# The last eight gate tiles move from between the delta levels to in front of the delta chain

## What is computed

```
u = rms(x, norm_mix)
dn_qkv, dn_z, dn_b, dn_a, r_*, a_*, i_*, gate = split(u @ w_in)      # gate: 3 x 1024 columns
c = silu(causal_conv(dn_qkv)); q, k, v = split(c); q, k = l2norm(q), l2norm(k)
o_a = chunked_recurrence(q, k, v, g, beta, dn_s0)                    # delta rule
# in a chunk: a = I + strict_lower(k k^T * decay * beta); solve a @ [u, kcum] = [v*beta, k*beta*exp(G)]
#             w = u - kcum @ s;  o = qd @ s + qk @ w;  s = s*gt + kd^T @ w
h = x + w_o @ sum_n sigmoid(gate_n) * (branch_n @ w_branch_n)
y = h + conv_ffn(rms(h))
```

## Time and profile before

| | us |
|---|---|
| median of three executions | 3210.27 |
| the profiled execution, its own time | 3210.03 |
| its span, first to last instruction | 3208.2 |
| PE busy in the span | 2894.5 (90%) |
| DVE busy | 1485.8 (46%) |
| ACT busy | 1258.8 (39%) |
| POOL busy | 812.5 (25%) |
| mean granted TensorE clock | 0.918 of 2.4 GHz |

### The profile page before, as it was taken

How to read it: one execution, slowest core, us unless ns; L and a number is a source line. 1 busy time by engine, 2 the same in 40 slices (tenths; PEclk the granted TensorE clock), 3 DMA queues, 4 the chain that set the end, 5 groups by cost and what they waited for, 6 DMA issues and landing times. The chain is left out here.

```text
span 3208.2 us, 56817 instructions
## 1 busy us (share of the span) xinstructions
PE 2894.5 (90%) x22582; PEld 2719.8 (85%) x22582; DVE 1485.8 (46%) x2238; ACT 1258.8 (39%) x2255; POOL 812.5 (25%) x364
## 2 busy tenths in 40 slices
PE   4998999989986989999879999899889879899996
PEld 3998988888876979999868989788878769799995
DVE  2362855654433526436136448466444243461541
ACT  3431434751113435345244224367311053552542
POOL 1221222220000424444222213122100024244441
PEclk7998999999975989999979979999999589899998
DMA  5221324533323513232232222254333234123321
GB/s 166 80 83 57 100 88 146 165 104 100 96 67 95 187 53 93 73 106 68 79 96 82 64 79 91 97 183 126 116 90 97 79 121 151 53 81 98 87 83 58
DMA packets 366310, 315.86 MB, mean 98 GB/s; under 512 B 42710, under 2 KB 314488, under 8 KB 365494
## 3 DMA queue, kind: packets, MB, share of 16 engines
q10 hardware_dynamic: 257332, 188.09, 19.7%
q1 hardware_dynamic: 108706, 124.05, 13.1%
HBM read 273.70 MB, written 38.38 MB: 97 GB/s over the span
## 5 line engine op out<-in xcount | busy, mean ns | idle before, releaser
L757 POOL TENSOR_TENSOR w_lo<-w_raw,w_hi 128x1024 fp32r<-128x1024 f32 (+2 forms) x360 | 812.3, 2257 | 2339.0 <-ACT w_hi L1343 2339.0
L764 PE MATMUL big<-uhi,w_hi 128*128 128x272 f32 x3968 | 1208.4, 305 | 62.7 <-DVE ulo L1845 24.4
L766 PE MATMUL big<-uhi,w_lo 128*128 128x272 f32 x3968 | 1165.0, 294 | 0.0
L765 PE MATMUL big<-ulo,w_hi 128*128 128x272 f32 x3968 | 1159.6, 292 | 0.0
L764 PEld LDWEIGHTS big<-uhi,w_hi 128*128 128x128 f32 x3968 | 765.2, 193 | 123.3 <-issue 71.8
L765 PEld LDWEIGHTS big<-ulo,w_hi 128*128 128x128 f32 x3968 | 768.2, 194 | 3.7 <-issue 1.9
L766 PEld LDWEIGHTS big<-uhi,w_lo 128*128 128x128 f32 x3968 | 764.9, 193 | 0.0
L1343 ACT ACTIVATE w_hi<-w_raw 128x1024 fp32r<-128x1024 f32 (+2 forms) x360 | 343.8, 955 | 346.1 <-PE big L766 317.3
L764 PE MATMUL big<-hhi,w_hi 128*128 128x272 f32 x704 | 204.8, 291 | 1.4 <-DVE hlo L2376 1.4
L766 PE MATMUL big<-hhi,w_lo 128*128 128x272 f32 x704 | 203.6, 289 | 0.0
L765 PE MATMUL big<-hlo,w_hi 128*128 128x272 f32 x704 | 202.9, 288 | 0.0
(11 more groups left out here) (351 smaller groups left out, 4111.9 us busy)
## 6 DMA issues: line engine op xcount, KB each, us to landing
w_raw<-in_w_in ACTq DMA_DIRECT2D x66, 1024.0 KB, 5.6
w_raw<-in_w_up ACTq DMA_DIRECT2D x88, 512.0 KB, 5.0
kpage<-in_cache_k SPq DMA_DIRECT2D x128, 256.0 KB, 3.1
w_raw<-in_w_down ACTq DMA_DIRECT2D x32, 704.0 KB, 4.8
d_conv<-in_cache_v SPq DMA_DIRECT2D x64, 256.0 KB, 2.7
d_pad<-in_cache_v SPq DMA_DIRECT2D x64, 256.0 KB, 2.6
gate_dram<-gate_raw ACTq DMA_DIRECT2D x48, 272.0 KB, 2.2
sig<-gate_dram SPq DMA_DIRECT2D x48, 272.0 KB, 3.4
```

The source lines that it names most:

```text
L757: po.tensor_tensor(split_view(lo, t), tile_of(t), split_view(hi, t).bitcast(F32), ALU.subtract).then_inc(w_lo.sem, w_lo.next(t))
L764: pe.matmul(out, wh, xh, start=start, stop=False)
L765: pe.matmul(out, wh, xl, start=False, stop=False)
L766: return pe.matmul(out, wl, xh, start=False, stop=stop)
```

## The change

The last eight gate tiles join `DN_PHASE` behind the last delta projection. There they are ordinary dense tiles, each at one go, in alternating slots (`DN_SLOT`), with `store_gate` behind each. `TILES`, and so the order in which weights are loaded and split, stays the same. The generator and all `advance` calls go from the delta chain, and both `store_gate` calls from ACT's part of it. Nothing stands in their place. `silu_of(11)` moves from behind the whole list to ahead of the first added gate copy. The value pages stay where they are. `key_slot` does nothing at the added positions, since all key pages are done by then. The core of the diff:

```diff
-DN_PHASE = dn_with_gates('dn0', 'dn1', 'dn2', *GATES[4:6]) + dn_with_gates('dn3', 'dn4', 'dn5', *GATES[6:8])
-DELTA_GATES = [(u, i) for u in GATES[8:12] for i in range(2)]
+DN_PHASE = dn_with_gates('dn0', 'dn1', 'dn2', *GATES[4:6]) + dn_with_gates('dn3', 'dn4', 'dn5', *GATES[6:8]) \
+    + [(u, i) for u in GATES[8:12] for i in range(2)]
@@ TensorE
-        gates = gate_steps(DELTA_GATES)
         for c in range(5):
@@ the prologue, after two value pages
-                advance(gates, 8)
@@ in each level, after Y and after YT
-                    advance(gates, 1)
@@ after the levels, after kc, after the first part of do
-                advance(gates, 3)
-                advance(gates, 5)
-                advance(gates, 2)
@@ ACT, in the loop over DN_PHASE
+            if p == DN_AT[-1] + 1:
+                silu_of(11)
             if u in GATES:
                 store_gate(u, j, p % 2)
@@ ACT, the chain
-        silu_of(11)
         for c in range(5):
-                if c < 4 and s == LEVELS[4]:
-                    store_gate(*DELTA_GATES[2 * c], 1)
-                store_gate(*DELTA_GATES[2 * c + 1], 1)
```

More of the change, by code:

```diff
@@ L217 @@
     + [(u, i) for u in UNITS[UIDX['ak0']:UIDX['dn0']] for i in range(2)] + DN_PHASE \
-    + [(u, i) for u in UNITS[UIDX['dn5'] + 1:] for i in range(2)]
+    + [(u, i) for u in UNITS[UIDX['br00']:] for i in range(2)]
 TIDX = {t: i for i, t in enumerate(TILES)}
@@ L1203, in _ @@
                     value_page(next(pages))
-                    advance(gates, 1)
-            if c < 4:
-                advance(gates, 3)
             pe.wait_ge(X[0].drained, X[0].at(('YT', c, levels[-1])))
```

## The result

The changed kernel took **3245.97 us**, the median of four executions (3242.96 to 3249.27), beside 3210.18 for the kernel before on the same chip (four, 3208.25 to 3211.61). The ratio is 1.0112, 95% interval 1.0095 to 1.013: slower by 36 us. The forecast was 3236, range 3219 to 3258. The profiled execution is the longest of the four, 3249.27 us with a span of 3247.5, 3.3 us above its median; differences between profiles are read with that in mind.

What follows compares the result with a forecast made beforehand. TensorE was busy nearly everywhere but not always the bound; within levels, TensorE, ACT and DVE take turns. 48.3 - 8.3 - 20.0 - 12.1 = +7.9 us a layer; 3210.03 + 15.8 + 10 (clock) = 3236 us, range 3219 to 3258.

Steps and rivals of the forecast that it cites:

- Part 1: Ahead of the chain: eight added dense gate tiles at 6.04 us each, +48.3 us a layer.
- Part 2: The head, before the first level: TensorE's idle and half-clock start go, 8.3 us instead of 16.6, -8.3 us a layer.
- Parts 3 and 4: Levels and chunk end: gate steps on the path go, 5.0 us a chunk over four chunks, -20.0 us a layer.
- Part 5: Prologues of chunks 1 to 3: 9.7 us instead of 15.7, 14.3 and 11.3, without POOL's w_lo and gate steps, -12.1 us a layer.
- Part 6: TensorE's clock in prologues and around kc: four falls to half clock taken, +10 us, range 0 to +30.
- A: Chunk 4 and sample states: clock stays up behind the chain, so not slower, 3189 us; 4%.
- A2: Chain: no clock dips, and the 0.20 us idle ahead of the gate step goes too, 3218 or 3215 us; 11%.
- B: Levels: without gate steps the clock falls, 2.5 us in each of 56 levels, +140, near 3365 us; 5%.
- C: Level and chunk ends: something other than gate steps orders them, the chain gives half, +20, near 3256 us; 8%.
- D: Dense tiles: ACT is crowded, a tile takes 7 us instead of 6.04, +15 in both layers, 3251 us; 5%.

Runs made afterwards that it cites:

- the kernel with the held clock: The changed kernel plus 30 matmuls a chunk whose results nobody reads, ahead of dvT, ahead of the first level and around kc: 3231.8 us.
- the two runs that move it: Four tiles in free chain places, next weights prepared right behind the gate store: 3184.4 us; the kernel before, preparation moved two levels into the next chunk: 3191.81 us.
- the kernel of before with the deferred preparation: The kernel before, with the weight preparation after the second store of chunks 0 to 2 moved two levels into the next chunk: 3191.81 us.
- the run on chunk 4: The kernel with four gate tiles in free chain places, plus 42 matmuls in chunk 4 whose results nobody reads: 3186.83 us.
- the kernel with five tiles: Against the kernel with four gate tiles in free chain places, a fifth put in the chain, three left dense: 3175.15 us.

## Why the prediction was right in sign and range, and 10 us short

- **Part 1, the dense tiles: right.** 8 x 6.04 is 48.3; measured 48.1 (702.41 to 750.55).
- **Part 2, the head: right.** From the first grow matmul to the first Y 7.65 us, forecast 8.3. With part 1 the stretch ahead of the first Y grew by 39.2 us, forecast 40.0.
- **Parts 3 and 4, levels and chunk end: right, slightly too high.** Read in the kernel with the held clock, chunk 3 to dS is 36.57 us where it was 41.1: 4.5 us, forecast 5.0. A level gives 0.38 us, where I kept 0.42. The 0.20 us that TensorE's queue takes behind a page is still there, now ahead of Y.
- **Part 5, the prologues: right.** dS to Y 9.65 to 9.75 us, forecast 9.7; 12.2 us a layer, forecast 12.1. That POOL's `w_lo` was the cause of the 2.41 us copy is shown by the two runs that move it, together with the ends of the copies.
- Parts 1 to 5 together: 39.2 - 4 x 4.54 - 12.2 = +8.8 us a layer, +18 in both, where the forecast was +15.8.
- **Part 6, the clock: the step that was mis-sized.** I took four falls at 2.5 us, +10, from gaps of 1 and 1.9 us against one of 2.91 that had made the clock fall. The kernel before had shown a second such case that I did not use: the clock fell behind a gap of 2.88 us in chunk 2's prologue (0.50 from 823.86 to 827.27), and not behind the 1.38 us of chunk 3's, where eight gate steps follow. Now it fell twelve times, the upper bound that I had written down, and all eight prologues were among them. The price of one was below mine: the first levels cost 1.2 to 2.6 us more than 6.03, and dw to dS 1.4 to 1.6 more than 2.77, 1.7 on the mean. In the profiled execution that makes 20 us (243.1 and 239.8 against 222.4 + 8.8 each). By medians it is at least the 14 us of the run with the held clock. The count was wrong by a factor of three, and the price too high by a half; the two partly made up for each other.
- By medians +36 is then 18 from parts 1 to 5, some 14 to 15 from the clock, and 3 left over. Outside the two stretches seven of the eight profiles of kernels with added dense tiles are 1 to 5 us longer than that of before, and one is 1.5 us shorter; which instructions those are was not found. Part of it is scatter: the end of the last delta projection of layer 1, ahead of everything that was edited, lies between 699.9 and 704.3 us in the ten profiles, at 699.9 in that of before and at 703.3 in the kernel of before with the deferred preparation, which has no dense tile more. And the interval of the ratio reaches from 30 to 42 us.

**The rivals.** A, the clock stays up behind chunk 3: it did not (0.55 against 0.53). What it would be worth there is not shown; the run on chunk 4 held it in two short levels only and gained 1.4 us in them. A2, no change: out, the 0.20 us idle stayed and the falls came. B, the clock falls in the levels: out in its size, since all levels behind the first ran at 1.00; the first level of every chunk did run at half clock in part, behind the waits of its prologue. (The prediction puts B's sum "some 140 us above mine"; its own figures, 3365 and 3236, are 129 apart.) The section of the Trainium skill that I set against the change ("TensorE: Matmul & The Clock Gate", "Loop structure matters more than you think", bursts with waits run cold) was worth more than the 5% I gave B, though what it describes is a long wait for a DMA ahead of every matmul: the trace agrees in the prologues, where the waits are short ones for ACT and DVE, 0.93 and 1.82 us, and not in the levels, where they are 0.39. C and D: out, Y to Y and the tiles came out as computed.

The argument had one blind spot behind it. It asked what the tiles cost as dense tiles and what the chain gives back, and treated the free places as of no account, since they saved nothing. They were worth the most: steps in free places make a tile cost nothing, and in these runs they held the clock besides. Of the 32 steps a chunk, 20 can lie in places that cost nothing or almost nothing; that is the kernel with five tiles.

## What to carry to other kernels

When filler work is taken out of a chain of small dependent steps, split it by place before it is priced: where another engine's copy ends last the filler is free and stays, where TensorE itself is late it costs its own length and goes. Count as well the gaps that are left: waits of about 1 and 2 us with little between them were enough for the clock to fall in every chunk, and each fall cost 1.2 to 2.6 us. And look at what the filler makes other engines prepare: here one weight preparation a chunk on POOL, beside the prologue, cost the kernel before half of what reordering the tiles could win.

## What the hardware showed beyond that

- The granted clock fell to 0.50 in each prologue with a gap of 0.86 or 0.93 us, four transposes and two value pages, and a gap of 1.82 us. It stayed at 1.00 when TensorE had 4 gate steps in the second gap and nothing in the first, and with 5 and 12 unread matmuls in the two. Behind kc it fell with waits of 0.49 and 1.59 us around one group of matmuls, in four of eight chunks in one kernel and in eight of eight in another with the same order there.
- Some DVE instructions are held until a POOL instruction beside them has ended. A copy of 0.43 us took 1.93 and ended 0.29 us behind `w_lo`, and a product of two SBUF tensors, 0.69 us, took 1.53 and ended 0.55 us behind it. The Trainium skill says so in "SBUF — State Buffer", section "SBUF: two separate sides": the port pair that both use is locked for a whole instruction and the other engine blocks. Both pairs of rows agree with that. It holds not for every DVE instruction: the subtraction from `d_t`, one of whose operands lies in PSUM, took its 0.69 us inside a `w_lo` (743.88 in the rows above). That fits with what the runs show: the same preparation costs nothing beside a level, and up to 2 us beside the prologue.
